# A one-core transformer-step kernel: a new order of the opening's matrix products, tile 1's attention four picks later, and GpSimd's powers one to twelve gathers later

## What is computed

```python
def peer(h, w_query, keys1, keys2, exp_u, exp_v):
    q = (h @ w_query).reshape(T, PEER_HEADS, 2, D_PHALF)       # 8 heads, halves of 128
    v1, i1 = lax.top_k(q[:, :, 0] . keys1, 16);  v2, i2 = lax.top_k(q[:, :, 1] . keys2, 16)
    cand_s = v1[..., :, None] + v2[..., None, :]               # 256 pairs
    top_s, sel = lax.top_k(cand_s, 16);  e_idx = cand_i[sel];  gate = softmax(top_s)
    act = gelu(einsum('thkd,td->thk', exp_u[e_idx], h))
    return einsum('thk,thkd->td', gate * act, exp_v[e_idx])    # 16 experts a head and token
```

## Time and profile before

| what | us |
|---|---|
| median of 3 timed runs (lowest, highest) | 1145.2 (1144.81, 1145.22) |
| the profiled execution | 1146.64 |
| its span, first to last instruction | 1144.6 |
| busy in the span: PE, DVE, POOL, ACT | 865.9, 784.9, 538.3, 453.8 |
| first gather issued at | 109.87 |
| bytes moved | 456.58 MB, of which gathers 402.68 MB |

### The profile page before, as it was taken

The page is one execution under the profiler, slowest core; times in us unless marked ns, Lnnn a source line. Parts: engine busy times, 40 slices in busy tenths (PEclk is TensorE's granted clock), DMA queues, the critical chain, the costliest instruction groups (busy, mean ns, idle before and its releaser), DMA issues.

```text
span 1144.6 us, 12068 instructions
## 1 busy us (share of the span) xinstructions
PE 865.9 (76%) x3879; PEld 398.9 (35%) x3884; DVE 784.9 (69%) x2005; ACT 453.8 (40%) x1423; POOL 538.3 (47%) x437
## 2 busy tenths in 40 slices
PE   8999989997896958684687677677676666666556
PEld 6748754443232424241233342233223222211111
DVE  2325877866677888896666785857877777667554
ACT  2121444433444334543554663343433333333334
POOL 0002536553555555563543454555564555556442
PEclk9999989999999888897888999698888889977788
DMA  9902999999999999999999999999999999999996
GB/s 375 410 2 70 415 427 424 426 426 429 425 427 426 426 428 420 411 410 406 426 428 424 425 426 428 405 427 426 426 428 426 426 427 426 427 427 427 426 428 265
DMA packets 66790, 456.58 MB, mean 399 GB/s; under 512 B 8227, under 2 KB 10019, under 8 KB 15526
## 3 DMA queue, kind: packets, MB, share of 16 engines
q0 software_dynamic: 55888, 402.68, 83.9%
q1 hardware_dynamic: 10694, 52.87, 11.3%
q10 hardware_dynamic: 144, 0.26, 0.1%
HBM read 451.49 MB, written 3.24 MB: 397 GB/s over the span
## 4 chain that ended last, share of the span: by engine, by line
DMA 47%; PE 28%; DVE 9%; POOL 6%; ACT 5%; issue 4%; SPq 0%; POOLq 0%; DVEq 0%
DMA rows<-in_uv,ids 38%; PE ps L598 28%; DMA wt<-in_uv,ids 6%; DVE rows L2043 5%; POOL rows L537 4%; POOL work L520 2%; ACT wt L1249 2%; ACT work L1249 1%; DMA rows<-in_w_qi 1%; DMA wt<-in_uv,last_ids 1%; ACT wgt L1249 1%; DMA wt<-in_w_q 1%; PE ps L601 1%; ACT L1249 1%; DVE wt L2043 1%
## 5 line engine op out<-in xcount | busy, mean ns | idle before, releaser
L537 POOL DMA_INDIRECT rows<-in_uv,ids x352 | 399.1, 1134 | 442.1 <-PE ps L598 357.4
L598 PE MATMUL ps<-rows,work 128*64 128x512 f32 x1416 | 416.5, 718 | 239.1 <-ACT work L1249 236.1
L2043 DVE CUSTOM_DVE_ANT_0 rows<-rows,wt 128x1024 f32<-128x1024 f32 x226 | 276.6, 1224 | 164.7 <-DMA rows<-in_uv,ids 160.7
L1249 ACT ACTIVATE zact<-zdot 128x1 f32<-128x1 f32 x354 | 71.5, 202 | 489.7 <-DVE zdot L2043 483.1
L598 PEld LDWEIGHTS ps<-rows,work 128*64 128x64 f32 x1416 | 97.1, 153 | 476.4 <-ACT work L1249 329.4
L598 PE MATMUL ps<-wt 128*128 128x128 f32 (+6 forms) x719 | 195.2, 473 | 26.0 <-ACT wt L1249 24.2
L2043 DVE CUSTOM_DVE_ANT_0 rows<-rows,masks 128x1024 f32<-128x1024 f32 x128 | 157.1, 1229 | 67.5 <-DMA rows<-in_uv,ids 63.0
L598 PEld LDWEIGHTS ps<-wt 128*128 128x128 f32 (+2 forms) x724 | 98.4, 187 | 102.4 <-issue 59.1
L1249 ACT ACTIVATE work<-pair,wgt 128x64 f32<-128x64 f32 x354 | 123.1, 348 | 11.5
L1249 ACT ACTIVATE wgt<-zact,gates 128x1 f32<-128x1 f32 x354 | 104.3, 295 | 11.5
L598 PEld LDWEIGHTS ps<-work,wt 128*128 128x128 f32 (+1 forms) x664 | 83.6, 201 | 47.3 <-issue 46.9
(11 more groups left out here) (178 smaller groups left out, 727.4 us busy)
## 6 DMA issues: line engine op xcount, KB each, us to landing
wt<-in_w_q SPq DMA_DIRECT2D x7, 2048.0 KB, 15.9
rows<-in_uv,ids POOLq DMA_INDIRECT x352
rows<-in_w_out SPq DMA_DIRECT2D x2, 2048.0 KB, 32.4
wt<-in_w_out SPq DMA_DIRECT2D x2, 2048.0 KB, 11.3
wt<-in_ckv SPq DMA_DIRECT2D x16, 256.0 KB, 12.0
x<-in_x SPq DMA_DIRECT2D x5, 512.0 KB, 9.0
rows<-in_w_qi SPq DMA_DIRECT2D x1, 2048.0 KB, 13.5
wt<-in_w_qa SPq DMA_DIRECT2D x1, 2048.0 KB, 12.8
```

The costliest lines, as they stand in the source:

```text
L537: pool.indirect_dma_start(row[s], None, a["uv"], bass.IndirectOffsetOnAxis(ap=ids[:, own(n // KP).start + n % KP:own(n // KP).start + n % ...
L598: return nc.tensor.matmul(out, lhsT, rhs, start=start, stop=stop)
L1249: return nc.scalar.activation(*args, **kw)
L2043: V.tensor_tensor_reduce(row[s][:, 0:D], row[s][:, 0:D], h2r[t][:, n % 2, :], 1.0, 0.0, ALU.mult, ALU.add, zdots[s]).then_inc(dotted, 1)
```

## The change

1. The opening's fillers become single products: `index_queries` now counts products (0 to 32). `h2_t(0)` is cut in two halves of four transposes (`h2_t0(e)`), each waiting for its own half of h2 instead of for all of it and the square; that last wait moves to `h2_take` of ScalarE and VectorE. Fillers behind `query(0)` shrink from 8 products to 2.
2. `spread_out(0)` stands after `sums_1(0)` instead of after `sums_1(1)`, and `dots_1(3)` behind it.
3. `y_start(0)` leaves the opening for pick 12, and the first `add_experts` opens the accumulator in its place. Tile 1's first attention steps stand four picks (or two) later: `scores_1` at 6 and 8, `prob_t1`/`values_1` at 18, 22, 26, the exponentials at 15 and 16 instead of both at 11. Four of VectorE's eight ranking rounds move behind picks 0 to 3. Three projections and part of `retention_1` stand 2 to 4 picks later.
4. GpSimd's powers stand 1 to 12 gathers later, and `query(16)`, `h2_t(2)` and its norm two picks later.

```diff
-        if n == 48:
+        if n == 49:
             group_rstd(1)
-        if n == 81:
+        if n == 83:
             take_rstd(H2_STAT[1])
-        if n == 124:
+        if n == 126:
             group_rstd(2)
-        if n == 140:
+        if n == 152:
             take_rstd(Y_STAT[0])
-        if n == 223:
+        if n == 225:
             take_rstd(H2_STAT[2])
...
+            def h2_t0(e):
+                pe.wait_ge(gained, e + 1)
+                for c in range(4 * e, 4 * e + 4):
+                    last = tr(ps[:, 3 * e, (c % 4) * P:(c % 4 + 1) * P], h2[:, c * P:(c + 1) * P])
+                if e:
+                    last.then_inc(h2t_ps, 1)
...
-            index_queries(1, 6, 0, 1)
-            h2_t(0)
-            index_queries(1, 6, 1, 2)
+            h2_t0(0)
+            index_queries(1, 6, 0, 3)
+            h2_t0(1)
+            index_queries(1, 6, 3, 7)
             query(0)
-            index_queries(1, 6, 2, 3)
+            index_queries(1, 6, 7, 9)
             query_scores(0)
-            index_queries(1, 6, 3, 4)
+            index_queries(1, 6, 9, 32)
...
             sums_1(0)
+            spread_out(0)
             dots_1(3)
             sums_1(1)
-            spread_out(0)
...
             def background():                      # ScalarE
-                yield from until(11)
+                yield from until(15)
                 exps_1(0)
+                yield
                 exps_1(1)
...
+                for r in range(TOPK[1] // 2, TOPK[1], 8):      # VectorE, attention_1
+                    whole(score_round(score1, r, TOPK[1], 0))
+                    yield from score_round(score1, r, TOPK[1], 1)
+                set_bias(bias1, score1)
```

More of the change, by code:

```diff
@@ L628, in keys_values, with index_queries @@
                 natural(t, w_kv, 6 + t % 2, NKV).then_inc(kv_ps, 1)
[L630 to L635, removed]
+            def index_queries(t, bank, i0, i1):
+                for i in range(i0, i1):
+                    j, c = divmod(i, KC)
+                    last = mm(ps[:, bank, j * P:(j + 1) * P], w_qi[:, c, j * P:(j + 1) * P], hT(t, c), c == 0, c == KC - 1)
+                if i1 == 4 * KC:
                     last.then_inc(qi_ps, 1)
@@ L880, in add_experts @@
                         s = ring(n + j)[0]
-                        last = mm(ps[64 * j:64 * j + 64, Y_BANK[n // (HP * KP)] + e, :], diag[s], row[s][:, D + e * 512:D + (e + 1) * 512], False, stop)
+                        last = mm(ps[64 * j:64 * j + 64, Y_BANK[n // (HP * KP)] + e, :], diag[s], row[s][:, D + e * 512:D + (e + 1) * 512], n == 0, stop)
                 last.then_inc(acc, 1)
@@ L986, in retention_1 @@
             def retention_1():
-                yield from until(26)
+                yield from until(28)
                 pe.wait_ge(rotated, 2)
@@ L1145, in attention_1 @@
             def attention_1():
+                yield from until(6)
                 scores_1(0)
-                yield from until(6)
+                yield from until(8)
                 scores_1(1)
-                yield from until(14)
+                yield from until(12)
+                y_start(0)
+                yield from until(18)
                 prob_t1(0)
-                yield from until(18)
+                yield from until(22)
                 values_1(0)
                 prob_t1(1)
-                yield from until(22)
+                yield from until(26)
                 values_1(1)
@@ L1219, in later_background @@
                 yield from later_out(2, 8)
-                yield from until(ATT2 + 66)
+                yield from until(ATT2 + 68)
                 h2_t(2)
@@ L1535, in background @@
                 square(H2_STAT[2], x[:, 2, :], h2)
-                yield from until(ATT2 + 69)
+                yield from until(ATT2 + 71)
                 h2_take(2)
@@ L1872, in _ @@
             then(V.tensor_tensor(score1[:, P:2 * P], ps[:, 3, P:2 * P], bar[:, 0:P], ALU.add), scored)
-            for r in range(0, TOPK[1], 8):
+            for r in range(0, TOPK[1] // 2, 8):
                 whole(score_round(score1, r, TOPK[1], 0))
                 whole(score_round(score1, r, TOPK[1], 1))
-            set_bias(bias1, score1)
             clock = Clock()
@@ L1906, in retention_1 @@
             def retention_1():
-                yield from until(23)
+                yield from until(25)
                 dve.wait_ge(cs_again, 16)
@@ L2008, in attend_2 @@
                 mean_square(H2_STAT[2])
-                yield from until(ATT2 + 65)
+                yield from until(ATT2 + 67)
                 normed(h2, H2_STAT[2], 2, g2b, hready)
-                yield from until(ATT2 + 69)
+                yield from until(ATT2 + 71)
                 h2_take(2)
```

51 lines of the change are left out of this document (25 added, 26 removed).

## The result

The changed kernel takes **1148.55 us** (median of 8 runs, 1147.9 to 1152.13) where the kernel before takes 1145.17 (8 runs, 1143.93 to 1145.42): a ratio of 1.0036, 95% interval 1.0027 to 1.0045. It is slower by 0.36% by the ratio (4.1 us; the medians differ by 3.4), and 2.65 us above the top of the forecast's range. The profiled execution took 1147.9, the fastest of the eight, with a span of 1146.1.

A forecast was written before the change was run, and what follows sets the result against it. The prediction took the DMA stream at 427 GB/s, and when it starts, as the bound. Terms -2.67 + 0.4 + 0.3 + 0.2 + 0.5 gave about -1.3 us, from 1145.2 to 1143.9 us; range 1142.3 to 1145.9.

The forecast's parts named there:

- The bound: Whole kernel: after the opening, one stream of gathers and loads at 427 GB/s that never stops sets the end.
- The opening: Start: new fillers, halves of h2 and the spread's place bring the first gather 2.67 us earlier, near 107.2.
- The gap: Gathers 8, 10, 12 and load_q(1): the earlier stream's shorter queue runs thin, 0 to 2.2 us, taken as 0.4.
- The start's gain: Opening: the stream starts 2.67 us earlier, counted as -2.67 in the sum.
- Attention four picks later: Tile 1's attention steps, picks 11 to 34: later exponentials, two more table loads; terms taken as 0.3 and 0.2 us.
- the steps of picks 14 to 34 are packed closer: Past 170 us: nearly full TensorE may not follow, making gathers late; 0 to 2.3 us, taken as 0.2.
- The gap of 155 to 170: SyncE's load over x and load_q(2) wait for y_start(0), 1 to 4 us later; 0 to 1.5 us, taken as 0.3.
- The powers: GpSimd's later powers: free, except group_rstd(2), which makes VectorE wait 4 us at o_normed; 0 to 3.5 us.
- The term of 0.5: Cost taken for VectorE's wait for group_rstd(2) near 457.6, by the queue's end between 471 and 473.
- The start's gain is given back: Rival: TensorE sets the pace, so the earlier stream runs dry between 140 and 250; 1144.7 to 1145.6 us, chance 0.18.
- The slower rival: VectorE's wait for group_rstd(2) at 457.6 is not covered, gathers 130 to 135 late; 1147.5 to 1149.6 us, chance 0.08.

The follow-up runs named there:

- e2: Kernel before with only GpSimd's six powers at their later gathers; 1145.02 us, ratio 0.9995.
- e1: Kernel before with only the new opening (fillers, halves of h2, the spread's place), y_start staying in the opening; 1145.38 us, ratio 0.9996.
- e14: Changed kernel with tile 1's attention steps and GpSimd's powers back at their old places, y_start at pick 12; 1144.8 us, ratio 0.9998.
- e5: Changed kernel with tile 1's attention steps back at their old picks, y_start at pick 12; 1143.68 us, ratio 0.9985.
- e6: Changed kernel with both exponentials in one batch and VectorE's rotation at pick 27 instead of 25; 1143.83 us, ratio 0.9988.
- e13: e6 with the three later projections moved two picks later, so no pick holds two; 1143.37 us, ratio 0.9982.
- e15: e13 with group_rstd(2) back at gather 124; 1143.41 us, ratio 0.9985.
- e8: Kernel before with only a pick put between the two batches of exponentials at pick 11; 1145.57 us, ratio 1.0001.
- e4: Changed kernel with both batches of tile 1's exponentials in one piece at pick 15; 1144.9 us, ratio 0.9994.
- e11: e6 with group_rstd(2) back at gather 124; 1143.46 us, ratio 0.9993.

## Why the prediction was wrong

**The bound** was read right, with one fault. I wrote that the stream "never stops", while the earlier trace rows shows 406 to 411 GB/s in slices 17 to 19. These are the places in which the changed kernel got part of its loss back and in which e2's dip vanished.

**The opening** held. The spread came at 106.20 (106.19 worked out), the first gather at 107.21 (107.2), gather 8 at 126.48 (126.5), `load_q(1)` at 138.85 (138.9), gather 12 at 140.99 (141.0). `load_q(1)` landed in 8.14 us (8 to 10) and `query(2)` began at 147.42 (147.5 to 149). The gap, taken as 0.4 within 0 to 2.2, was about 1.2: the lead went from +3.1 at 120 to +1.9 at 155. Only some 0.4 of it is at `load_q(1)` and gather 12, the place that I had worked out. The other 0.9 us are gone by 125, at gather 4, which I had not put on the list: 28 fillers stand ahead of it instead of 24, so it is issued at 117.13, 0.3 us later than before, while the stream started 2.67 us earlier. The windows at the two places:

```profile
120.00:121.00 1.00, 1.00 (x8) 0.92 (x8) 0.97 (x5) 0.51 (x2) 0.30 (x1) 1.00 0.49 180
141.00:142.00 1.00, 0.83 (x4) 0.34 (x6) 1.00 (x3) 0.87 (x5) 1.00 (x1) 1.00 0.72 295
```

In e1, without `y_start` moved, the lead at 155 was -0.2, and in e14, which has it moved, +2.0. Their times (1145.38 and 1144.8) do not show that difference, and e14's lead is gone by 170. The start's gain appears in a time only in kernels with later powers beside it (e5, e6, e13, e15), and whether that is their merit or scatter is the open point above.

**The step that failed** is *Attention four picks later*, in the term "the steps of picks 14 to 34 are packed closer", 0 to 2.3 us, taken as 0.2. It measured 7.0 in the stream, of which some 3 came back; undoing these steps (e5) takes 0.51% off the time. Three things went wrong in it:

- I wrote that "two more table loads come" and gave them no price. They lengthen TensorE's wait by 2.84 us (e8; e4 against the changed kernel).
- I wrote that `add_experts(12)` no longer waits behind the exponentials. I did not ask which pick stands behind them now. It is pick 16, with less of TensorE's work beside the exponentials: its wait is 8.91 us (6.07 without the split), where pick 12 of the kernel before has 2.48.
- VectorE's rotation moved by two picks, from 23 to 25, while the projection that feeds it moved by four, from 14 to 18. The order of the two lists shows that, and I never set them side by side. It is the wait of 4.65 us, and 2.97 on TensorE.

The term was also bounded by the wrong quantity. TensorE's 35.81 of 40 us leaves 4.2 us free, and I asked if more work would fit in. No work was added; idle time was, 7.7 us between 155 and 204, against a queue I had put at 4.5 to 8 us. The gap of 155 to 170, taken as 0.3 within 0 to 1.5, was 0 in the changed kernel, though its mechanism is real: the load over x came 14.8 us later than before (162.62 against 147.79) and `load_q(2)` 0.2, not 1 to 4, and in other executions up to 2.6 us were lost there (e14).

**The powers** went as forecast: a wait of 3.81 us at `o_normed(2)` (about 4 worked out), GpSimd's power behind gather 126 and the gate's. It costs up to 2.2 us of the stream at 480 (e2, e5; in the changed kernel the lead is -4.9 at 440 and -4.8 at 480), and nothing at the end that the runs can tell. One reading was off: I put the queue's end between 471 and 473, but by the earlier trace rows gather 129 lands at 465.32 + 10.23 = 475.55. The term of 0.5 took its size from that.

**The rivals.** "The start's gain is given back" named the right place, a stream that runs dry between 140 and 250, with 1144.7 to 1145.6 us. Its mechanism was idle time that TensorE fails to lose; the real one is idle time that it gains, so its time was 3 us too low. The slower rival's time, 1147.5 to 1149.6, contains the result, but by another mechanism: e2, and e11 beside e6, show no cost of its wait at the end.

## What to carry to other kernels

When a group of steps moves by so many picks, list each producer and consumer with its old and new pick, and look for the pair whose distance has shrunk; ask which waiting instruction now stands behind the moved one. Then ask what work the waiting engine has beside the moved step in its new place. An edit that is free alone need not be free beside others that drain the same queue: the split cost nothing in the kernel before (e8) and 0.42% in the changed one, so a price measured alone does not carry over. A slice that is a few per cent below full is room in which later losses disappear, and deserves a look before a term is carried to the end.

## What the runs showed of the hardware

Each table load on ScalarE is 1.28 us, and the next instruction starts right behind it (162.40 and 163.69); two more of them (2.56 us) lengthened TensorE's wait by 2.84. The Trainium skill, page "ScalarE: Activation LUTs", section "What ACT_TABLE_LOAD costs", has the same load (about 1283 ns) and adds 1380 ns of draining, 2.66 us for each switch. The trace agrees with the load and shows no such drain; by the page two more switches would have cost 5.3 us, an estimate.

TensorE's clock fell behind its waits. It stood from 199.34 to 202.31 at a granted clock of 1.00; the next eight records then took 2.95 us instead of 1.94, and the granted clock is 0.50, the level of 1.2 GHz, in the whole of the second window, before it rises to 2.4 GHz again. Windows of the changed kernel:

```profile
202.00:204.00 2.00, 1.69 (x6) 0.59 (x8) 1.97 (x8) 0.66 (x3) 0.00 (x0) 0.78 1.01 426
204.00:206.00 2.00, 2.00 (x8) 0.81 (x4) 2.00 (x10) 0.44 (x2) 0.46 (x1) 0.50 1.01 426
```

So the wait of 2.97 us cost TensorE at least 1.0 more in the products behind it. In e4 the same wait was followed by eight records in 3.63 us; in e6, where it was 1.34, the six records behind it took 2.84 us, close to the 2.74 they take elsewhere. Behind the wait of 8.91 us, the granted clock was 0.50 from 174 to 178, and the 16 records lost 2.65 us (6.53 against 3.88).
